# A two-stack transformer forward pass on one core: the gated feed-forward products of three layers taken by Strassen's method, with the weights' sums made in DRAM

## The reference

```python
def conv_ffn(x, w_up, conv_w, conv_b, w_down):      # layers 0 and 1
    h = x @ w_up                                    # 1024 -> 2 * 2816
    hc = conv_b
    for j in range(CONV_W):                         # causal, width 3
        hc = hc + hp[:, j:j + L] * conv_w[j]
    u, g = jnp.split(hc, 2, axis=-1)
    return (jax.nn.silu(g) * u) @ w_down
...
    f = rmsnorm(h, norm_ffn_g[i])                   # the last block
    h = h + (jax.nn.silu(f @ w_gate[i]) * (f @ w_up[i])) @ w_down[i]
```

## Time and profile before

| | |
|---|---|
| Time, median of three | 2309.79 us (2309.68 to 2310.2) |
| The profiled execution's own time | 2309.27 us |
| its span, first to last instruction | 2307.3 us |
| TensorE busy | 2287.0 us, 15423 matmuls |
| VectorE busy | 1285.3 us |
| ScalarE busy | 909.8 us |
| GpSimd busy | 34.5 us |
| DMA | 197.47 MB moved, 86 GB/s over the span |

### The profile page before, as it was taken

One profiled execution on the slowest core, in us unless ns is written; L12 is line 12 of the kernel. 1 busy time (PEld: TensorE's weight loads), 2 busy tenths in 40 slices (PEclk: granted clock), 3 DMA queues, 4 the chain that ended last, 5 costly groups with the idle time before them and its releaser, 6 DMA issues.

```text
span 2307.3 us, 36725 instructions
## 1 busy us (share of the span) xinstructions
PE 2287.0 (99%) x15423; PEld 2038.2 (88%) x15423; DVE 1285.3 (56%) x2258; ACT 909.8 (39%) x1566; POOL 34.5 (1%) x75
## 2 busy tenths in 40 slices
PE   9999999999999999999999999999999999999998
PEld 7798999999997898999899788978898888888887
DVE  5356576446643465766366566869455455443443
ACT  5356544224333465543144443223244444221232
POOL 2000000000000000000000000000000000000001
PEclk9999999999999999999999999999999999999999
DMA  4221223222312221323223222223222232332331
GB/s 137 92 72 47 86 83 100 87 80 92 110 58 74 93 61 43 102 92 107 77 92 109 80 75 74 91 85 98 92 65 65 65 101 92 100 110 74 100 109 55
DMA packets 57910, 197.47 MB, mean 86 GB/s; under 512 B 8545, under 2 KB 12547, under 8 KB 57747
## 3 DMA queue, kind: packets, MB, share of 16 engines
q1 hardware_dynamic: 55827, 189.73, 25.6%
q0 software_dynamic: 1344, 4.36, 0.6%
q10 hardware_dynamic: 576, 1.05, 0.1%
HBM read 192.98 MB, written 2.13 MB: 85 GB/s over the span
## 4 chain that ended last, share of the span: by engine, by line
PE 93%; DVE 3%; ACT 2%; issue 1%; DMA 0%; POOL 0%; SPq 0%; ACTq 0%; DVEq 0%; POOLq 0%
PE G L1079 76%; PE G L1153 7%; PE X L1365 1%; PE X L1320 1%; PE X L1447 1%; PE X L1343 1%; DVE wL L1950 1%; PE X L1431 1%; PE X L1148 1%; ACT wH L1489 1%; PE X L1416 1%; PE X L1079 1%; PE X L1403 0%; PE X L1279 0%; PE X L1375 0%
## 5 line engine op out<-in xcount | busy, mean ns | idle before, releaser
L1079 PE MATMUL G<-aH,wH 128*128 128x264 f32 (+2 forms) x2992 | 759.0, 316 | 4.0 <-DVE wL L1950 3.6
L1079 PE MATMUL G<-aL,wH 128*128 128x264 f32 (+2 forms) x2992 | 738.1, 309 | 0.0
L1079 PE MATMUL G<-aH,wL 128*128 128x264 f32 (+2 forms) x2992 | 737.5, 309 | 0.0
L1489 ACT ACTIVATE wH<-raw 128x512 fp32r<-128x512 f32 (+3 forms) x477 | 386.9, 829 | 666.6 <-PE G L1079 612.1
L1950 DVE TENSOR_TENSOR wL<-raw,wH 128x512 fp32r<-128x512 f32 (+3 forms) x477 | 443.7, 941 | 207.1 <-ACT wH L1489 205.1
L1079 PEld LDWEIGHTS G<-aH,wH 128*128 128x128 f32 x2992 | 488.0, 189 | 43.5 <-issue 9.9
L1079 PEld LDWEIGHTS G<-aH,wL 128*128 128x128 f32 x2992 | 485.6, 188 | 29.4
L1079 PEld LDWEIGHTS G<-aL,wH 128*128 128x128 f32 x2992 | 486.2, 188 | 26.9 <-issue 0.2
L2102 DVE TENSOR_TENSOR hT<-G,hT 128x528 f32<-128x528 f32 (+1 forms) x83 | 58.1, 700 | 215.8 <-PE G L1079 215.8
L1079 PE MATMUL G<-hidH,wH 128*128 128x264 f32 (+1 forms) x528 | 140.7, 321 | 1.4 <-DVE hidL L2186 1.4
L1079 PE MATMUL G<-hidL,wH 128*128 128x264 f32 (+1 forms) x528 | 141.1, 322 | 0.0
(11 more groups left out here) (348 smaller groups left out, 2689.9 us busy)
## 6 DMA issues: line engine op xcount, KB each, us to landing
raw<-weights SPq DMA_DIRECT2D x276, 512.0 KB, 3.5
raw<-weights SPq DMA_DIRECT2D x48, 704.0 KB, 4.0
raw<-weights SPq DMA_DIRECT2D x12, 384.0 KB, 3.1
negc<-sums POOLq DMA_DIRECT2D x16, 264.0 KB, 4.4
out_t<-hT SPq DMA_DIRECT2D x16, 128.0 KB, 1.8
raw<-weights SPq DMA_DIRECT2D x14, 128.0 KB, 2.1
hT<-x_t ACTq DMA_DIRECT2D x4, 256.0 KB, 4.8
hT<-x_t SPq DMA_DIRECT2D x4, 256.0 KB, 7.0
```

Of the source, the lines that this page charges most:

```text
L1079: done = e.matmul(m.pair(i)[0:M, bank, 0:n], a[:, k, 0:M], b[:, kx, lo - t0:lo - t0 + n], start=(k == 0 and c == 0), stop=(k == nk - 1 and ...
L1489: e.activation(m.high(i)[:, c], m.raw[:, r, c], ACT.Copy).then_inc(s.w_hi, 1)
```

## The change

For 7 of the 11 pairs of the first half and all 11 of the second in layers 0 and 1 (8 and 11 in the last block), the two chunks of a pair are replaced by seven products of Strassen's method. A pair is seen as a 2 x 2 matrix of blocks: rows are the up tile and the gate tile, columns the first and the last four blocks of 128 inputs; the activations are likewise 2 x 2, the input halves by the two halves of the tokens (264, 258 or 256 each). One of the seven products is 4 blocks x 3 matmuls of half the tokens.

- Sums of the activations (`sum7`, VectorE) are made once for a layer, and the activations have to be normed first (`norm7`, VectorE, eight tiles; before, the norm's scale was multiplied in by `evac`). Each of the seven operands is split into a high and a low part (`high7`, ScalarE, and `low7`, VectorE, 128 x 1056). This is put between the matmuls of the plain pairs, from the second pair on; the parts of the last three operands go into the first three steps of the Strassen stage.
- Sums of the weights are made in DRAM, by DMAs that GpSimd issues (`make`): a copy of a block of tiles and then an accumulating DMA onto it, each waiting for the one before, 48 in all over 6 half stages. They are 1.84 to 2.88 MB each. A load of such a weight waits for its sum.
- The results are added up partly in PSUM, where one product accumulates onto another, and partly by three copies and a fourth on ScalarE (`p1st`, `p5th`, `u2nd`, `c21`) and three additions on VectorE (`c11`, `c22`, `c12`). Convolution, SiLU, product and parts follow as before, one piece in a step (`conv7`, `silu7`, `gate7`, `hidh7`, `hidl7`).
- The weights of a product are 128 x 512: the two buffers of `wH`/`wL` are used as five, and the four of `raw` as eleven.

```diff
+SEVEN = {0: 4, 1: 4, 2: 3}
+STAGE = {0: (0, 264), 1: (12, 258), 2: (16, 256)}
+SUMS = (5, (1, 5)), (6, (5, 3)), (4, (6, 2)), (7, (5, 3))
+EVERY = 3.5, 5
...
+        if role[0] == "seven":
+            if ROLE[i - 1][0] != "seven":
+                run = 1
+                while ROLE[i + run][0] == "seven":
+                    run += 1
+                k = -run % 5
+            at, k, n = 512 * k, (k + 1) % 5, n + n % 2
+        else:
+            at, n = WMAX * (n % NW), n + 1
...
+    def background(i):
+        n = state["made"]
+        state["work"] += 0.25 if ROLE[i][0] == "seven" else 1
+        if n < len(MADE) and state["work"] >= (2 + EVERY[0] * n if n < 16 else 2 + EVERY[0] * 16 + EVERY[1] * (n - 16)):
+            step("make", n)
+            state["made"] += 1
...
+    def seven():
+        last = ()
+        while ROLE[state["next"]][0] == "seven":
+            i = state["next"]
+            _, f, half, jj, p = ROLE[i]
+            if ROLE[i - 1][0] != "seven":
+                flush()
+            state["next"] += 1
+            background(i)
+            while state["split"] < len(PLAN) and WAS.get(state["split"], -1) < i and ROLE[state["split"]][0] != "out":
+                step("split", state["split"], 0, 1)
+                state["split"] += 1
+            if pieces:
+                step(*pieces.popleft())
...
+            step("prod7", f, half, jj, p)
+            step({1: "p1st", 2: "c11", 5: "p5th", 6: "u2nd", 7: "c22", 3: "c12", 4: "c21"}[p], f, half, jj)
+            if p == 3 and f < 2:
+                pieces.append(("conv7", f, half, jj, 1))
+            if p == 4:
+                pieces.extend([("conv7", f, half, jj, 0)] if f < 2 else [])
+                pieces.extend(("%s7" % what, f, half, jj) for what in ("silu", "gate", "hidh", "hidl"))
+            yield
+        while pieces:
+            step(*pieces.popleft())
...
+    def operands(f):
+        out = [("norm7", f, j) for j in range(8)] + [("high7", f, 1), ("low7", f, 1), ("high7", f, 2), ("low7", f, 2)]
+        for p in 5, 6:
+            out += [("sum7", f, p), ("high7", f, p), ("low7", f, p)]
+        return out + [("sum7", f, 7), ("sum7", f, 3)]
...
+    def prod7(f, half, jj, p):
+        out = X[:, 2 + g, 0:n] if p == 2 else m.G[g][:, 1 if p in (5, 3) else 0, 0:n]
...
+        elif p == 7:
+            e.wait_ge(s.sums_act, SUMS_ACT[("u2nd",) + key])
...
+        e.wait_ge(s.w_lo, SPLIT_DONE[i][0])
...
+        for k in range(4):
+            for c, (a, b) in enumerate(((wh, xh), (wh, xl), (wl, xh))):
+                done = e.matmul(out, a[:, k, :], b[:, k, :], start=(p in (1, 2, 5) and k == 0 and c == 0),
+                                stop=(k == 3 and c == 2), skip_group_check=p not in (1, 2, 5))
...
+    def make(n):
+        to, size, (at, of_sums), add = MADE[n]
+        out = SU[to:to + size].rearrange("(p n) -> p n", p=128)
+        block = (SU if of_sums else W)[at:at + size].rearrange("(p n) -> p n", p=128)
+        if n:
+            e.wait_ge(s.made, 16 * n)
+        if add:
+            e.dma_start(out, block, accum_op=ALU.add, max_dma_last_dim=8192).then_inc(s.made, 16)
+        else:
+            e.dma_start(out, block).then_inc(s.made, 16)
...
     def load(i):
...
+        if i in READY:
+            e.wait_ge(s.made, 16 * READY[i])
+        src = (SU if i in READY else W)[WEIGHT_AT[i]:WEIGHT_AT[i] + 128 * SIZE[i]]
+        e.dma_start(m.raw(i), src.rearrange("(p n) -> p n", p=128)).then_inc(s.ring[RING[i]], 16)
```

438 lines of the change are left out of this document (369 added, 69 removed).

## The result

The changed kernel takes 2330.66 us (median of four, 2327.17 to 2333.32), the kernel before 2309.99 in the same rounds: a ratio of 1.009, 95% interval 1.0078 to 1.0102. It is slower by 0.9%, where 2291 us, faster by 0.8%, was forecast. The profiled execution took 2330.64 us, its span is 2329.4.

What follows compares the result with a forecast made beforehand. TensorE was taken as the bound: its matmuls' count and spacing, and new stops. Against 72.5 us removed stood 53.3 us added (13.2 + 24 + 4.5 + 8.6 + 3), 19.2 us less: 2291 us, range 2268 to 2318.

Steps and rivals of the forecast that it cites:

- The stream: TensorE's matmuls in the gated halves: fewer or shorter ones take 72.5 us off.
- Item 1: Start of first halves: TensorE waits for the last plain pair's chain before the second product's split; 13.2 us added.
- Item 2: Plain pairs: making operands leaves VectorE late, lengthening the stop at the first halves' start; 24 us added.
- the prediction's second choice: VectorE's lateness from the operands shows before the first halves' start, as waits for the split or the scaling.
- Item 3: Start of second halves: the first product's split waits for TensorE's end of the last down chunk; 1.5 us three times, 4.5 us.
- Item 5: Steady part of the Strassen stages: VectorE 9.6 us a pair against TensorE's 10.3, so nothing added, by a hair.
- Rival B: Strassen stages: VectorE bounds the steady part, costing 11 to 20 us, 2302 to 2311 us in all; chance 0.17.
- over nine tenths: Sign that the main forecast is right: VectorE's busy share in the stages of layers 0 and 1.
- Item 4: Ends of the halves: VectorE's last pieces and the second down chunk's split come late; 8.6 us added.
- Item 7: Weight sums made in DRAM by GpSimd's DMAs: they land before layer 0's second half, about 487 us, and cost nothing.
- rival C: DMA engines: loads wait beside long rows, or sums are slow, so TensorE waits for weights; 2310 to 2330 or 2406 us; chance 0.20.
- Item 6: Clock behind TensorE's stops: 5 us or more may cost nothing or some 2 us; 3 us for layers 0 and 1 together.

Runs made afterwards that it cites:

- no_low_parts: raw_end without VectorE's low parts of the seven operands, TensorE reading the high part in their place: 2302.3 us, ratio 0.9971.
- raw_end: Changed kernel with stages' first places in raw chosen so the first down chunk's buffer is not the last product's: 2314.1 us, ratio 1.0020.
- no_sums: Changed kernel without the DMAs that make the weight sums, plain weights loaded in their place: 2313.1 us, ratio 1.0017.
- stops: Kernel before with twenty waits of TensorE for GpSimd added in the gated halves of layers 0 and 1: 2430.7 us, one execution.
- together_short: together with the sums' copies and accumulating DMAs in rows of 2 KB: 2293.8 us, ratio 0.9932.
- five_plain: raw_end with one more plain pair ahead of each first Strassen stage: 2321.3 us, ratio 1.0054.
- together: raw_end with freed splits ahead of the last plain pair's remaining steps, and sums kept from out-projections and stages' last three pairs: 2300.6 us, ratio 0.9963.

## Why the prediction was wrong

- **The stream** was right: 72.5 us forecast, 73.8 found.
- **Items 1 and 2** (starts of the first halves and operands): 37.2 us forecast, 34 of idle time found. Item 1's chain is there: 5.4, 6.6 and 2.8 us at the second products against 5.2, 5.2 and 2.8, and it stayed when VectorE's low parts were left out (no_low_parts). Item 2 shows in the plain pairs, 18.5 us in three layers against 24. That it stands there and not at the stage's start was the prediction's second choice. That the low parts, and so VectorE's work, make it is shown by no_low_parts.
- **Item 3**: 4.5 us forecast, three stops of 1.6 found.
- **Item 5**, the steady part: nothing was added, as forecast. 0.123 us a matmul in 505 to 619 us. Rival B fell. VectorE was busy for 101.52 of 114 us, 0.89, where over nine tenths was the sign.
- **Item 4**, the ends, was mis-sized by its mechanism: 8.6 us forecast, some 16 found. "By the durations of items 1 and 2 the tenth's low part is done 7.9 us after the last product" was reckoned on VectorE, and gave 1.3 us in layer 0, where 2.0 was forecast. In layer 1 and the last block the stop was a load into a buffer of `raw` that the last product still held (raw_end); the prediction had looked at the places in `wH` and `wL` only.
- **Item 7** failed: "in time, cost nothing". The sums were in time: the sixteenth was issued at 311.76 us and the next, which waits for it, at 331.01, against the 487 us allowed. But with them on another queue the loads beside them landed three to five times as late (256 KB after 9.2 to 9.6 us in place of 2.9, the out-projection's 128 KB after 11.2 in place of 2.3 in the kernel before), and TensorE stopped in the out-projections, which the prediction had not looked at since the change does not touch them. 11.9 us of idle time, and with the clock behind it 18.8; no_sums gave 17.5. This is rival C, by its first branch ("a load's row of 2 KB waits"), not at the place it named.
- **Item 6** failed most: "I put 3 us for layers 0 and 1 together". The clock fell twelve times between start and end, and 22 us lie at these falls, of 29 us in all by which matmuls came more slowly. The row of a 3.3 us stop passed at 1.00 was read as a sign that such stops may be free; in the run stops one of 3.4 us cost 1.6 to 1.8 more, and the row was the exception, two traces of sixteen. The prediction had itself counted eight further stops of 1.5 to 2.8 us and 24 us of lateness, and priced the clock for layers 0 and 1 as if for one or two stops. The Trainium skill, "TensorE: Matmul & The Clock Gate", section "HAM oscillation — how this bites in real kernels", has the rule that idle gaps between bursts bring the half-rate clock back; the trace agrees, with the table above, if not at every stop (3.00 us at 2077.40).

Forecast -19.2, found +22.1 in the span. Of the 41 us between them 26 are slower matmuls (29 found, 3 put for the clock; 22 of the 29 at its falls, some of the rest behind stops without a fall), 12 the stops in the out-projections and 7 the ends; the starts and the stream were 3 and 1 us better than forecast. The gain is real, and could be kept: with the same arithmetic together_short runs at 0.9932 of the kernel before. What is open is how the stops of the plain pairs would be avoided, since spreading did not do it and five_plain moved the buffers as well, and what the rest of together_short's idle time, 60 us against 20 before, is worth with its clock.

## What to carry to other kernels

Where the clock fell behind a stop of TensorE of 2.8 us or more, that cost 1.6 to 2.9 us beyond the stop's length in the run stops, and 1.4 to 3.0 us at a fall in the changed kernel. So several stops of 3 us in a kernel that had none are to be priced at half as much again or more, though single ones passed free. One stop that passed free in one trace says nothing of the next. Background DMAs are to be checked against the tightest loads anywhere in the time they run, not against the part that they serve, and tried in short rows, which gained 7 us here between together and together_short. Where buffers are laid over others of another size, look at the load that comes next after the change of size: its buffer may be the last to come free.
